# A reordered transition between two phases of a decoder layer: the threshold of a top-256 selection moved behind the second norm, GpSimd's short sums and weight remainders put side by side, and eight page loads given to SyncE

## What is computed

```python
def trunk_layer(x, ...):
    h = rms_norm(x, norm1_g)
    u, q, k, v, iq, ik, iw = project(h, pos, w_in, q_norm_g, k_norm_g)
    ya, pool_state = pool_mix(u, pool_prefix, pos0, w_pool, pool_scale)
    yb = attend(q, k, v, iq, ik, iw)     # the indexer's 256 best keys per query
    x = x + jnp.concatenate([ya, yb], axis=-1) @ w_o
    x = x + peer(rms_norm(x, norm2_g), w_pq, sub_keys, expert_u, expert_v)
    return x, k, v, ik, pool_state

def dsa_block(q, iq, iw, qpos, idx_keys, k_sel, gather_kv):
    s = jnp.einsum('bqhd,bld->bqhl', iq, idx_keys)
    score = jnp.einsum('bqhl,bqh->bql', jax.nn.relu(s), iw)
    top_val, top_idx = lax.top_k(score, k_sel)           # k_sel = 256 of 1028 for the samples
    logits = jnp.einsum('bqhd,bqkd->bqhk', q, k_rows) * (HEAD_DIM ** -0.5)
    return jnp.einsum('bqhk,bqkd->bqhd', softmax(logits), v_rows)

def peer(h, w_pq, sub_keys, expert_u, expert_v):
    q = (h @ w_pq).reshape(N, PEER_HEADS, 2, PEER_HALF)
    s = jnp.einsum('nhcd,hckd->nhck', q, sub_keys)
    ...                                                   # product-key top 16, gelu, sum of rows of expert_v
```

## Time and profile before

| | us |
|---|---|
| median of 3 runs | 981.35 |
| lowest, highest | 981.3, 982.72 |
| the profiled execution, device time | 981.55 |
| its span, first to last instruction | 980.1 |
| TensorE busy | 958.2 |

### The profile page before, as it was taken

How to read it: one execution, slowest core, us unless ns; L and a number is a source line. 1 busy time by engine, 2 the same in 40 slices (tenths; PEclk the granted TensorE clock), 3 DMA queues, 4 the chain that set the end, 5 groups by cost and what they waited for, 6 DMA issues and landing times.

```text
span 980.1 us, 19215 instructions
## 1 busy us (share of the span) xinstructions
PE 958.2 (98%) x6440; PEld 835.3 (85%) x6440; DVE 777.5 (79%) x1805; ACT 558.6 (57%) x1092; POOL 438.6 (45%) x328
## 2 busy tenths in 40 slices
PE   5999999999999999999999999999999999999998
PEld 2347879899999999999999998888888888888887
DVE  2569987269999948999999976777888878788873
ACT  2023354454445559999999975654555555555552
POOL 4643465145788776776777770011212211131200
PEclk9999999999999999999999999999999999999999
DMA  9635748668855554444445456797888888888872
GB/s 330 149 109 160 238 139 308 209 226 316 280 176 175 180 185 150 152 161 160 150 155 165 151 173 217 257 337 283 300 300 305 299 279 296 303 304 303 291 263 94
DMA packets 75424, 221.24 MB, mean 226 GB/s; under 512 B 11301, under 2 KB 23725, under 8 KB 74964
## 3 DMA queue, kind: packets, MB, share of 16 engines
q1 hardware_dynamic: 60812, 179.12, 53.7%
q0 software_dynamic: 12800, 40.36, 13.3%
q10 hardware_dynamic: 1744, 0.92, 0.4%
HBM read 217.41 MB, written 3.14 MB: 225 GB/s over the span
## 4 chain that ended last, share of the span: by engine, by line
PE 86%; DVE 4%; DMA 4%; ACTq 2%; ACT 2%; issue 2%; SPq 0%; DVEq 0%
PE psum L1123 33%; PE psum L1059 22%; PE psum L1060 12%; PE psum L1071 3%; PE psum L1055 3%; PE psum L603 3%; PE psum L872 2%; ACTq L402 1%; PE psum L873 1%; DMA w_raw<-expert_v 1%; DMA rows_in<-expert_u,eidx 1%; PE psum L581 1%; DMA w_raw<-expert_ut 1%; DVE work L1825 1%; PE psum L887 1%
## 5 line engine op out<-in xcount | busy, mean ns | idle before, releaser
L1630 POOL TENSOR_TENSOR w_lo<-w_raw,w_hi 128x1024 fp32r<-128x1024 f32 x116 | 279.1, 2410 | 124.1 <-ACT w_hi L1170 123.9
L1059 PE MATMUL psum<-h_split,w_hi 128*128 128x256 f32 x1792 | 327.0, 284 | 1.3 <-issue 1.3
L1060 PE MATMUL psum<-h_split,w_lo 128*128 128x256 f32 x1024 | 289.4, 283 | 0.0
L1059 PEld LDWEIGHTS psum<-h_split,w_hi 128*128 128x128 f32 x1792 | 279.2, 192 | 2.6 <-issue 1.4
L1170 ACT ACTIVATE w_hi<-w_raw 128x1024 fp32r<-128x1024 f32 x214 | 224.9, 1051 | 39.4 <-DMA w_raw<-expert_ut 27.6
L1060 PEld LDWEIGHTS psum<-h_split,w_lo 128*128 128x128 f32 x1024 | 196.1, 191 | 0.0
L2145 DVE TENSOR_TENSOR w_lo<-w_raw,w_hi 128x1024 fp32r<-128x1024 f32 x98 | 120.5, 1229 | 54.7 <-ACT w_hi L1170 54.4
L1123 PE MATMUL psum<-w_hi,ag_hi 128*128 128x512 f32 x512 | 158.2, 390 | 0.4 <-DVE ag_lo L2152 0.4
L1123 PE MATMUL psum<-w_hi,ag_lo 128*128 128x512 f32 x512 | 158.0, 389 | 0.0
L1170 ACT ACTIVATE ag_hi<-store 128x256 fp32r<-128x256 f32 x128 | 53.2, 417 | 152.5 <-PE psum L1123 152.4
L1123 PEld LDWEIGHTS psum<-w_hi,ag_hi 128*128 128x128 f32 x512 | 95.8, 188 | 20.6 <-ACT w_hi L1170 0.8
(11 more groups left out here) (347 smaller groups left out, 1485.0 us busy)
## 6 DMA issues: line engine op xcount, KB each, us to landing
w_raw<-expert_ut SPq DMA_DIRECT2D x128, 512.0 KB
w_raw<-expert_v SPq DMA_DIRECT2D x86, 512.0 KB
raw_more<-expert_v SPq DMA_DIRECT2D x42, 512.0 KB, 4.8
w_slice<-w_pq_cols SPq DMA_DIRECT2D x32, 512.0 KB, 5.3
w_most<-w_in_blocks SPq DMA_DIRECT2D x8, 699.0 KB, 11.3
w_slice<-w_o_half SPq DMA_DIRECT2D x8, 512.0 KB, 4.7
v_cache<-cache_v POOLq DMA_DIRECT2D x64, 64.0 KB, 3.7
w_o_sb<-w_o_half SPq DMA_DIRECT2D x8, 512.0 KB, 6.1
```

What stands on the lines that cost most here:

```text
L1059: pe.matmul(out, w_hi[:, s, c, :], h_split[:, c, a], start=(c == 0 and a == 0), stop=False)
L1060: mm = pe.matmul(out, w_lo[:, s, c, :], h_split[:, c, 0], start=False, stop=(c == KC - 1), skip_group_check=wide)
L1630: pool.tensor_tensor(w_lo[:, s], w_raw[:, s], w_hi[:, s].bitcast(F32), ALU.subtract).then_inc(S["w_lo_ready"], 1)
```

## The change

It touches five instruction lists and no arithmetic.

- VectorE: `add_wo` is no longer evenly interleaved with `order`, and the last, `add_wo(7)`, comes ahead of the last `order`. `cut` goes from between `add_wo(5)` and `add_wo(6)` to behind the remainders of `h2`. `low_q(3)` goes ahead of `tally` and `low_q(4)` ahead of `admit`.
- GpSimd: the four `join_sq` and the three `low_q` follow each other, without the two groups of V loads that stood between them, and all its remaining V pages come behind.
- SyncE: the last eight V pages are loaded by it, behind `load_slice(11)` and ahead of the 18 row outputs. TensorE's `sample_values` waits for both counts.
- ScalarE: `high_q(2)` goes ahead of the root of the norm; `copy_q(0)`, `high_q(3)` and `copy_q(1)` go ahead of `copy_log(0)`, and `high_q(4)` between the two `copy_log`.
- TensorE: `rq(2)` goes ahead of `rs(0)`, and `rs(1)` follows `rs(0)`.

```diff
     K_SP = 44
+    V_SP = 8
...
             for q in range(4, 12):
                 load_slice(q)
+            sp.wait_ge(S["log_p_psum"], 2)
+            page_loads(sp, DB * NPG - V_SP, cache_v, v_cache[:].rearrange("p b n d -> p (b n d)"), HD, S["v_in_sp"],
+                       V_SP)
             sp.wait_ge(S["zp_copied"], 8)
...
-                pe.wait_ge(S["v_in"], 16 * DB * NPG)
+                pe.wait_ge(S["v_in"], 16 * (DB * NPG - V_SP))
+                pe.wait_ge(S["v_in_sp"], 16 * V_SP)
...
             rq_first()
+            rq(2)
             rs(0)
-            for r in range(2, 5):
+            rs(1)
+            for r in range(3, 5):
...
                 if i in (3, 5):
                     high_q(i // 2 - 1)
+            high_q(2)
...
-            high_q(2)
+            copy_q(0)
+            high_q(3)
+            copy_q(1)
             copy_log(0)
+            high_q(4)
             copy_log(1)
-            for r in range(3, 7):
+            for r in range(5, 7):
+                copy_q(r - 3)
                 high_q(r)
-                copy_q(r - 3)
...
-            join_sq(0)
-            v_loads(V_FIRST, 4)
-            join_sq(1)
-            join_sq(2)
-            join_sq(4)
-            low_q(0)
-            low_q(1)
-            v_loads(V_FIRST + 4, 4)
-            low_q(2)
-            v_loads(V_FIRST + 8, DB * NPG - V_FIRST - 8)
+            for i in (0, 1, 2, 4):
+                join_sq(i)
+            for r in range(Q_FIRST):
+                low_q(r)
+            v_loads(V_FIRST, DB * NPG - V_SP - V_FIRST)
...
-            for i in range(1, 5):
-                add_wo(i)
-                order(2 * i - 2)
-                order(2 * i - 1)
-            add_wo(5)
-            cut(0)
-            add_wo(6)
-            add_wo(7)
+            for i, stages in enumerate(((0, 1), (2, 3), (4,), (5,), (), (6,), (7,))):
+                add_wo(i + 1)
+                for stage in stages:
+                    order(stage)
...
+            cut(0)
+            low_q(3)
             tally(0)
-            low_q(3)
+            low_q(4)
             admit(0)
-            for r in range(4, 7):
-                low_q(r)
+            low_q(5)
+            low_q(6)
```

## The result

| | before | after |
|---|---|---|
| median of 6 runs each, us | 982.41 | 986.32 |
| lowest and highest | 981.3, 983.23 | 984.39, 988.21 |
| the profiled execution, its span | 980.1 | 986.2 |
| TensorE busy in it | 958.2 | 961.7 |
| mean granted clock in it | 1.000 | 0.994 |

The ratio is 1.0043, with a 95% interval of 1.0027 to 1.0058: slower by 3.9 us at the medians, where 3.8 were forecast.

The account below looks back on a forecast made before the run. TensorE was taken to bound the kernel, busy 958.2 of 980.1 us. The sum was 981.55 + 5.17 (late `rq(3)`) - 0.74 - 0.65 (later waits) = 985.3 us, range 982.8 to 988.8.

Parts of the forecast that it names:

- The lock ahead of the norm: VectorE's last `order` stage waits for GpSimd's remainders of 2.35 us each; `h2` starts at 141.0, 1.1 us later.
- SyncE: Eight V pages (8.24 us) and row outputs (8.60) delay `load_slice(12)` to 150.25; called the term that decides.
- The slice's landing: The slice of `load_slice(12)` lands 3.66 us after its issue, at 153.9, as first in the queue.
- The wait ahead of `rs(0)`: TensorE stands still from 151.2 to 156.0 for ScalarE's copies of the logits; `rq(3)` starts 5.2 us later.
- rival 1: TensorE's clock falls behind the wait of 4.8 us, costing 2.5 us: 987.8; chance 0.19.
- What comes back: Later TensorE waits shrink, 0.74 us at `rs(2)` and half of 1.30 at `rs(7)`, leaving +3.8 us.
- the 0.74 at `rs(2)`: TensorE's wait ahead of `rs(2)` goes, since ScalarE now copies before it rounds: 0.74 us back.
- the 1.30: TensorE's wait at `rs(7)` for a late slice; freer queues give between nothing and 1.30 us back, half taken.
- Rival 3: Norm no earlier, SyncE not late, `rs(0)` follows `rq(2)` at 151.2: 980.5 us, no measurable change; chance 0.07.
- the term that decides: SyncE's V pages ahead of the row outputs make `load_slice(12)` late, so TensorE waits at `rs(0)`: +5.2 us.

Follow-up runs that it names:

- `e5_stage_behind`: Changed kernel with the last stage of `order` behind the remainders of `h2` and slice 2's remainder on VectorE instead of GpSimd: 1.0052 of the kernel before.
- `e1_pages_behind`: Changed kernel with SyncE's eight V pages behind `load_slice(13)` instead of ahead of the row outputs: 1.0066 of the kernel before.
- `e9_fill_both`: Changed kernel with products that serve nothing in both long TensorE waits, 26 ahead of `rq_first` and 37 between `rq(2)` and `rs(0)`: 1.0034 of the kernel before.
- the second profile: Profile of the changed kernel run once more, nothing altered, in a second comparison: ratio 1.0053 to the kernel before.
- `e6_pages_back`: Changed kernel with all V pages loaded by GpSimd again, none by SyncE: 1.0038 of the kernel before.
- `c_after`: The changed kernel itself run once more, nothing altered: 1.0053 of the kernel before, median 985.84 us.
- `e2_pages_alone`: Kernel before with only SyncE's eight V pages added ahead of the row outputs, taken from GpSimd: 1.0049 of the kernel before.
- `e8_rq3_first`: Changed kernel without SyncE's pages, both `copy_log` ahead of `high_q(4)`, last `order` stage and slice 2's remainder behind `h2`'s on VectorE, `rq(3)` ahead of `rs(0)`: 0.9962.
- `e10_stage_kept`: Changed kernel without pages on SyncE and with both `copy_log` ahead of `high_q(4)`, last stage of `order` still ahead of the norm: 1.0021 of the kernel before.

## Why the prediction was right, and where it was not

Times of after are given less 1.75.

1. **The lock ahead of the norm**: forecast `h2` at 141.0 with two operations of some 2.35 us; measured 140.6, 2.11 and 2.46. Right: the same operations take 0.28 in `e5_stage_behind`, where they stand behind GpSimd's remainders. The Trainium skill (SBUF — State Buffer, section "SBUF: two separate sides") has the shared port pair locked for a whole instruction; the rows agree, 0.28 against 2.11 and 2.46 us.
2. **SyncE**: forecast 8.24 for the pages; measured 143.13 - 135.05 = 8.1. Row outputs: forecast 8.60, as in before; measured 7.4 (143.13 to 150.5). I took a duration with a hiccup in it for the rule: in before's trace one of these DMAs, `pool_prompt`, took 1.70 us to issue and in after's 0.47, and single ones of 1.39 (`e1_pages_behind`) and 1.90 (`e9_fill_both`) stand against 0.42 to 0.48 for the same DMA otherwise. `load_slice(12)` went out at 148.8 instead of 150.25, 1.9 us behind its release where the forecast had 2.95, and in the second profile not behind it at all.
3. **The slice's landing**: forecast 3.66; measured 4.4. It was the first in its queue, but the second and third were issued right behind it, and V pages ran beside it; which of the two did it, if either, was not tested. It took 3.5 us in `e6_pages_back` and 3.6 in `c_after`, where three slices went out over 4.2 us and not over 2.25.
4. **The wait ahead of `rs(0)`**: forecast 4.8 from 151.2 to 156.0; measured 4.72, from 150.6 to 155.3. The slice's earlier issue and its slower landing, 1.5 and 0.7, left the copies 0.8 early, and `rq(2)` was 0.6 early too.
5. **The clock**, rival 1: forecast 2.5 if it falls, chance 0.19. In the first profile it fell, for 2.4 us. So the execution that was profiled was rival 1, less the 0.8 us of point 4, and some 1.2 us came back later: at `rs(8)` after is 5.6 late, at the end 986.2 - 980.1 - 1.75 = 4.35. The chance was too low: of the eleven waits of over 3 us behind the opening of the profiles here, all but one were followed by a fall. My remark that the record of the granted clock shows 1.00 over the opening products was a misreading: its first entry in before starts at 15.04 us, so it says nothing of them, and the slow products of the earlier trace rows end just there. What I had not priced at all is the first wait, 3.31 us ahead of `rq_first`. My text had TensorE's idle time as one wait of 4.8, since I followed `h2` to the end of `rq(2)` and never asked what covered the norm before.
6. **What comes back**: the 0.74 at `rs(2)` came back in full. Of the 1.30 I gave back half; in its place there is now a wait of 0.93 ahead of `rs(6)`, so 0.37.
7. **Rival 3 was wrong in its own working.** It had `rs(0)` follow `rq(2)` without a wait once SyncE isn't late, and gave 980.5. By my own numbers the slice, released at 147.3, lands at 151.0, and the copies end 2.1 us later at 153.1, 1.9 behind `rq(2)`. `e6_pages_back` shows just that, 1.93. I had read the change as a fault of SyncE, when two parts make it together: the order on ScalarE makes `rs(0)` wait for slice 4, by 1.9 us even where SyncE is not late, and the pages can make the slice later. Either cure alone was worth 1.5 us (pages) or some 4 (order).

The forecast called SyncE's lateness the term that decides. It decides in `e2_pages_alone` (4.8 us, a fall of the clock among them), where the order on ScalarE is the old one and `copy_q(1)` stands behind the slice. In the changed kernel the term that decides is the order: the pages' part is 0 to 2 us of a wait that is there without them.

So the chain that was forecast (pages, slice, `copy_log(1)`, `rs(0)`) is in the trace link by link, but +3.8 against +3.9 measured is good partly by luck: the sum had no fall of the clock in it and the measured runs have, while the slice went out earlier and the order alone would have made nearly 2 us of the wait.

## What to carry to other kernels

Before an instruction that waits for a late transfer is put ahead of another in an in-order queue, ask who waits for the other: here two swapped lines on ScalarE were worth some 4 us, and eight page loads put ahead of the slice on SyncE cost 4.8 us in the old order and nothing that can be told once the two lines were swapped back. Before work is moved off the path, ask what covered the idle time behind it; products that once hid a norm stop hiding it when they start earlier. And an edit should be priced against the next bound: the same 3.2 us of norm were worth nothing behind SyncE's slice, and up to 5.4 once the slice was cured. Last, an experiment that takes a suspect away should be looked at for what then sets the time: without the pages TensorE itself, slowed by its clock, released the slice late.

## What the runs showed of the hardware that I had not expected

- The granted clock falls behind much shorter waits than the one of 9.81 us at the start. Behind the wait of 3.3 us ahead of `rq_first` it fell in six of seven profiles that have that wait; behind 3.44, 3.92, 4.72 and 8.15 us each time. Behind waits of 1.3 to 3 us it fell sometimes: behind 1.39 (after), 1.82 (`e9_fill_both`, at 47.5), 1.93 (`e6_pages_back`), 1.97 and 2.67 (`e1_pages_behind`) and 2.85 (`e8_rq3_first`), and not, among others, behind 1.39 in before, 1.71 and 1.95 in `c_after`, 2.08 in `e10_stage_kept`, 2.78 in `e9_fill_both`. None followed the three waits that were filled with products. The Trainium skill (TensorE: Matmul & The Clock Gate, section "Part 1: The HAM clock gate (the "warmup" mystery)") has an idle engine fall and regain its clock after sustained work; the rows agree in that every fall ahead of the kernels' last few us stood behind a wait. Why 1.39 us was enough in one execution and not in another, no run here shows.
- The time of one and the same kernel scatters, and goes partly with the clock: the six runs of after lie between 984.39 and 988.21 with mean clocks of 0.992 (the slowest) to 0.997, twelve of `c_after` between 981.94 (0.996) and 991.96 (0.991). That difference of 0.005 could cost 4.9 of the 10 us; where the rest comes from is open. A loss of 4 us has to be looked at over several runs, and one profile shows one throw.
- Two operations of 0.28 us became 4.57 us together beside GpSimd's remainders: they end at 137.24 and 139.63 in after, and the remainders at 137.10 and 139.48. Here the meeting cost the rest of GpSimd's running instruction, and the second short operation paid it anew, since GpSimd's next remainder had started by then (137.06).
